# Spacing the operand tiles of three-pass matmuls in SBUF by 80 and 32 bytes

## Chip, cores and metric

The kernel runs as one program on one core of one Trainium2 chip. The metric is the device time of one execution in microseconds, the median of several runs.

## What is computed

The reference chains two transformer blocks over 256 tokens of width 1024, all in float32. The first block has two layers, each with a wide projection, top-k attention and a short convolution, an output mix and an MLP of width 4096 with a squared ReLU. The second has one layer with a windowed and a neighbourhood attention, and then PEER, a product-key retrieval over 128 x 128 experts:

```python
def first_block(...):
    for l in range(DEPTH):                      # 2
        u = rmsnorm(x, norm_mix[l])
        proj = u @ w_in[l]
        ...
        x = x + merged @ w_mix_out[l]
        u = rmsnorm(x, norm_mlp[l])
        x = x + jnp.square(jax.nn.relu(u @ w_mlp_up[l])) @ w_mlp_down[l]
    return rmsnorm(x, norm_final)

def second_block(...):
    ...
    x = x + gate1[:, None, :] * (mixed @ w_out[layer])
    h2 = modulate(rms_norm(x, norm2_g[layer]), shift2, scale2)
    x = x + gate2[:, None, :] * peer(h2, w_query[layer], sub_keys[layer],
                                      u_experts[layer], v_experts[layer])
    return rms_norm(x, final_g)
```

Almost all of the arithmetic is activations (256 tokens) times weights, and every weight is used once.

## The kernel before

**The stream.** All weights are packed on the host into 544 pieces of 128 x 1024 float32 (512 KB each) in the order of use. SyncE loads them into `raw`, a ring of `RING` = 4 slots (L560). For each piece ScalarE writes `w_hi`, the value rounded to the format of TensorE's fast fp32 path (L182), and VectorE writes `w_lo = raw - w_hi` (L187), three pieces ahead of TensorE. `w_hi` and `w_lo` are rings of 4 slots too.

**Three-pass matmuls.** `mm3` (L210 to L212) makes one product of split operands from three matmuls: high by high, high by low, low by high. The activations are split likewise: `u_hi`/`u_lo` hold eight tiles of 128 features x 256 tokens, `a_hi`/`a_lo` two such tiles, used in turn. TensorE meets two forms:

- `piece_b`: a 128 x 128 block of the ring is stationary and a tile of `u` moves, 256 columns, 24 matmuls a piece (8 tiles `k` by 3). The projections, the MLP's up, the queries and the experts' up have this form. The profile writes it as `bank<-u_hi,w_hi` (moving first, then stationary).
- `piece_a`, `expert_down`, `held_pieces`: 128 tokens of `a` (or of `u`, `o`, `mx`) are stationary and half a slot of the ring moves, 512 columns, 12 matmuls a piece. The MLP's down and the experts' down have this form: `bank<-w_hi,a_hi`.

Each matmul carries its own load of the stationary block (LDWEIGHTS, PEld in the profile). The order on every engine is written out by hand and tied by semaphores.

**Where the tiles lie.** The program lays its tiles one after the other in each partition of SBUF, each starting at a multiple of 32 bytes. These are the start addresses in the built program, as remainders by 64 bytes:

| tile | step between its parts, before | start mod 64, before | step, after | start mod 64, after |
|---|---|---|---|---|
| `raw` | 4096 | 0 | 4096 | 0 |
| `w_hi`, `w_lo` (slots 0 to 3) | 4096 | 0, 0, 0, 0 | 4176 | 0, 16, 32, 48 |
| `u_hi`, `u_lo` (tiles 0 to 7) | 1024 | 0 for all | 1056 | 0, 32, 0, 32, ... |
| `a_hi` (2 tiles) | 1024 | 0 | 1024 | 0 |
| `a_lo` (2 tiles) | 1024 | 0 | 1024 | 32 |
| `one_r` | - | 0 | - | 32 |
| `o_hi`, `o_lo`, `y_hi`, `y_lo`, `mx_hi`, `mx_lo` | 1024 | 32 | 1024 | 0 |

`o`, `y` and `mx` are the other activations that meet the ring: attention and convolution outputs before their output projections, and the merged branches. `one_r` is a column of ones that `keep_clock` (L273) multiplies by itself, both operands broadcast.

Of the kernel before, what the change touches and what calls it, by code (L numbers as in the profile page):

```python
# [9 lines left out]
F32R = mybir.dt.float32r  # L10
# [7 lines left out]
P = 128  # L18
T, D = 256, 1024
NT, KD = T // P, D // P  # L20
# [26 lines left out]
PIECE = 1024  # L47
RING = 4
AHEAD = 3
N_LAYER = 59 + 2 * KH  # L50
ADA_GROUPS = 6
ADA_RING = 4
# [2 lines left out]
N_QUERY = 2 * PH  # L55
N_PIECES = LAYERS * N_LAYER + N_MIXER2 + N_QUERY + 2 * PK
SEL_PIECES = 8
# [35 lines left out]
def build(nc, stream, x_in, gains2, gain_cols, conv_w, w_ada, b_ada, c_cols, kept_in, rope_in, na_mask_in,  # L93
          t5_in, t5_hot, rpb_pad, sinks, sub_keys, gain_out, out):
    ctx = ExitStack()
    with ctx:
        def sb(c, name, shape, dt=F32):
            return c.enter_context(nc.sbuf_tensor(name, shape, dt))
# [9 lines left out]


        raw = sb(ctx, "raw", [P, RING, PIECE])  # L110
        w_hi = sb(ctx, "w_hi", [P, RING, PIECE], F32R)
        w_lo = sb(ctx, "w_lo", [P, RING, PIECE], F32R)
        u_hi = sb(ctx, "u_hi", [P, KD, T], F32R)
        u_lo = sb(ctx, "u_lo", [P, KD, T], F32R)
        a_hi = sb(ctx, "a_hi", [P, 2, T], F32R)
        a_lo = sb(ctx, "a_lo", [P, 2, T], F32R)
        kept = sb(ctx, "kept", [P, 2 * P + PT + 2 * LAYERS * KD])
        ident, iota, iota16 = kept[:, 0:P], kept[:, P:2 * P], kept[:, 2 * P:2 * P + PT]
# [53 lines left out]
        def dyn(k):  # L172

            return at["quads"] * k
# [15 lines left out]
        def split(c):  # L190
            split_hi(c)
            split_lo(c)

        def next_piece(last=False):
# [3 lines left out]
            if not last:  # L198
                split(c + AHEAD)
            nc.tensor.wait_ge(s_split, dyn(RING) + (c + 1))  # L200
# [107 lines left out]
        def squares(src, junk, row, marks, tt):  # L308

            for n in range(2):  # L310
                cols = slice(n * 512, (n + 1) * 512)
                m = AC.go((marks[tt][n], junk_mark[0]), S.activation, junk, src[:, tt, cols], ACT.Square,
                          accum_out=st[:, row + n, tt:tt + 1])
                junk_mark[0] = m
            return m
# [18 lines left out]
        def held_pieces(count, lhs, acc, steps, whole=False, ahead=True):  # L334
# [4 lines left out]
            for tt in range(NT):  # L339
                for n in range(2):  # L340
# [10 lines left out]
                    next(steps, None)  # L351
            return list(range(c + AHEAD + 1, c + AHEAD + count))

# [282 lines left out]
        for k, b in enumerate((5, 0, 1, 2, 3, 6, 7, 4)):  # L636
# [6 lines left out]
            u_ready.append((m1, m))  # L643
        for c in range(1, AHEAD):
            split(c)
        for tt in range(NT):
            got_sums[0] = squares(x, space_junk, 5, x_marks, tt)
        for layer in range(LAYERS):
# [422 lines left out]
            if layer < LAYERS - 1:  # L1071
                u_ready, x_sums = added_and_turned(*last_downs, x, gains[:, layer + 1, :], 5, mlp_scale)
                got_sums[0] = squares(x, space_junk, 5, x_sums, 1)
                assert at["piece"] == (layer + 1) * N_LAYER
        ph1a.close()
# [1003 lines left out]
```

## Time and profile before

| | before |
|---|---|
| median of 3 runs | 1732.64 us (1731.53 to 1732.9) |
| span of the profiled execution | 1732.8 us |
| TensorE matmul busy | 1711.1 us, 99% of the span |
| VectorE busy | 1328.8 us, 77% |
| ScalarE busy | 925.9 us, 53% |
| bytes moved by DMA | 327.3 MB, mean 189 GB/s |

The span is that of the execution that the hardware profiler recorded. It stands 0.2 us from the median, so a sum made against the span can be read against the median. Matmuls overlap in the pipeline, so a matmul's duration says little: what counts is the distance between the starts of two that follow each other, here called the pitch.

### The profile page before, as it was taken

The numbers are of one execution on the slowest core, as the hardware profiler recorded it, in microseconds if no ns is written. First come the engines' busy times: TensorE is split into PE (matmuls) and PEld (weight loads), VectorE is DVE, ScalarE is ACT, GpSimd is POOL, SyncE is SP. The second block draws the span as 40 slices with busy tenths as digits, with TensorE's granted clock in tenths as the row PEclk, the third lists the DMA queues.
The fourth block names the chain that finished last, engine by engine and source line by source line (L and its number), as shares of the span: only waits on it lengthen the run. The fifth ranks groups of instructions, "written<-read, shape, count | busy, mean of one in ns | idle before, by whom it ended". The sixth has DMA issues, their size and how long they took to land.

```text
span 1732.8 us, 33390 instructions
## 1 busy us (share of the span) xinstructions
PE 1711.1 (99%) x11670; PEld 1580.1 (91%) x11670; DVE 1328.8 (77%) x2382; ACT 925.9 (53%) x1647; POOL 63.5 (4%) x112
## 2 busy tenths in 40 slices
PE   9999999999999999999999999999999999999997
PEld 8899899989999898999889999999999988888886
DVE  6986778778976787877775999987888766666666
ACT  5444544445454544455554555577777655555553
POOL 0000001000000122100000000000000000000000
PEclk9999999999999999999999999999999999999999
DMA  6556687755445699744344555554444455555554
GB/s 232 170 179 199 217 291 274 244 181 167 162 159 161 226 328 308 253 148 145 122 158 158 166 175 182 182 171 136 145 135 137 144 194 194 193 192 192 191 192 153
DMA packets 90123, 327.30 MB, mean 189 GB/s; under 512 B 11001, under 2 KB 11177, under 8 KB 89585
## 3 DMA queue, kind: packets, MB, share of 16 engines
q1 hardware_dynamic: 79056, 286.45, 49.3%
q0 software_dynamic: 9712, 34.36, 6.2%
q10 hardware_dynamic: 1264, 5.24, 0.8%
q8 instruction: 62, 1.02, 0.2%
q14 instruction: 29, 0.23, 0.0%
HBM read 323.88 MB, written 6.09 MB: 190 GB/s over the span
## 4 chain that ended last, share of the span: by engine, by line
PE 76%; DVE 18%; DMA 2%; issue 2%; ACT 2%; DVEq 0%; ACTq 0%; SPq 0%
PE bank L210 23%; PE bank L211 22%; PE bank L212 22%; DVE Z L87 6%; DVE w_lo L187 6%; PE bank L1769 3%; DMA raw<-stream 1%; DVE yc L87 1%; PE bank L281 1%; PE bank L1310 1%; ACT w_hi L182 1%; PE bank L481 1%; DVE work L87 1%; DVE rot L87 1%; DVE top L87 1%
## 5 line engine op out<-in xcount | busy, mean ns | idle before, releaser
L187 DVE TENSOR_TENSOR w_lo<-raw,w_hi 128x1024 fp32r<-128x1024 f32 x544 | 658.2, 1220 | 162.1 <-ACT w_hi L182 161.2
L182 ACT ACTIVATE w_hi<-raw 128x1024 fp32r<-128x1024 f32 x544 | 572.4, 1054 | 245.5 <-PE bank L212 163.2
L210 PE MATMUL bank<-u_hi,w_hi 128*128 128x256 f32 x2400 | 691.2, 288 | 1.7 <-DVE w_lo L187 0.8
L211 PE MATMUL bank<-u_lo,w_hi 128*128 128x256 f32 x2400 | 679.8, 283 | 0.0
L212 PE MATMUL bank<-u_hi,w_lo 128*128 128x256 f32 x2400 | 679.7, 283 | 0.0
L210 PEld LDWEIGHTS bank<-u_hi,w_hi 128*128 128x128 f32 x2400 | 460.9, 192 | 11.6 <-DVE w_lo L187 3.8
L211 PEld LDWEIGHTS bank<-u_lo,w_hi 128*128 128x128 f32 x2400 | 461.2, 192 | 2.2
L212 PEld LDWEIGHTS bank<-u_hi,w_lo 128*128 128x128 f32 x2400 | 460.7, 192 | 0.0
L210 PE MATMUL bank<-w_hi,a_hi 128*128 128x512 f32 x744 | 290.4, 390 | 0.0
L211 PE MATMUL bank<-w_lo,a_hi 128*128 128x512 f32 x744 | 290.1, 390 | 0.0
L212 PE MATMUL bank<-w_hi,a_lo 128*128 128x512 f32 x744 | 289.5, 389 | 0.0
L212 PEld LDWEIGHTS bank<-w_hi,a_lo 128*128 128x128 f32 x744 | 139.7, 188 | 29.5
L210 PEld LDWEIGHTS bank<-w_hi,a_hi 128*128 128x128 f32 x744 | 139.9, 188 | 27.6 <-issue 0.2
L211 PEld LDWEIGHTS bank<-w_lo,a_hi 128*128 128x128 f32 x744 | 139.9, 188 | 27.0
L1858 ACT ACTIVATE a_hi<-Z 128x256 fp32r (+1 forms) x126 | 52.7, 418 | 169.0 <-PE bank L212 167.2
L1860 DVE TENSOR_TENSOR a_lo<-Z,a_hi 128x256 fp32r<-128x256 f32 x126 | 53.6, 426 | 81.6 <-ACT a_hi L1858 81.6
L1758 ACT ACTIVATE rows_a<-rows_a,sel 128x128 f32<-128x128 f32 x256 | 81.1, 391 | 0.0
L1742 DVE TENSOR_TENSOR rows_a<-kept,sel 128x512 f32<-128x512 f32 x64 | 44.3, 691 | 36.5 <-PE bank L1769 36.4
L1605 ACT ACTIVATE Z<-bank 128x256 f32 (+1 forms) x68 | 26.1, 384 | 79.2 <-PE bank L212 78.9
L959 ACT ACTIVATE qT<-bank 128x256 f32<-128x256 f32 x64 | 24.5, 383 | 74.9 <-PE bank L212 74.7
L994 DVE SCALAR_TENSOR_TENSOR space<-gate,c_tmp,space 128x1024 f32 x42 | 53.8, 1280 | 0.4
L968 DVE CAST a_hi<-qT 128x256 fp32r<-128x256 f32 x60 | 18.0, 300 | 43.9 <-PE bank L212 42.9
(286 smaller groups left out, 1713.1 us busy)
## 6 DMA issues: line engine op xcount, KB each, us to landing
raw<-stream SPq DMA_DIRECT2D x544, 512.0 KB, 3.3
gate<-w_ada POOLq DMA_DIRECT2D x48, 512.0 KB, 6.4
t_rows<-t_by_distance POOLq DMA_DIRECT2D x8, 256.0 KB, 3.4
rpb_rows<-rpb_pad POOLq DMA_DIRECT2D x8, 224.0 KB, 3.9
bias_b<-rpb_rows POOLq DMA_DIRECT2D x16, 96.0 KB, 7.7
bias_a<-t_rows POOLq DMA_DIRECT2D x1, 1536.0 KB, 14.9
x<-x_in ACTq DMA_DIRECT2D x2, 512.0 KB, 5.8
gains_b<-gains POOLq DMA_DIRECT2D x1, 1024.0 KB, 9.0
```

The costliest lines, as they stand in the source:

```text
L87: return self.done(method(*args, **kw))
L182: nc.scalar.activation(w_hi[:, s, :], raw[:, s, :], ACT.Copy).then_inc(s_hi, 1)
L187: nc.vector.tensor_tensor(w_lo[:, s, :], raw[:, s, :], w_hi[:, s, :].bitcast(F32), ALU.subtract).then_inc(s_split, 1)
L210: M.matmul(o, lh, rh, start=start, stop=False, skip_group_check=True)
L211: M.matmul(o, lh, rl, start=False, stop=False, skip_group_check=True)
L212: return M.matmul(o, ll, rh, start=False, stop=stop, skip_group_check=True)
L994: nc.vector.scalar_tensor_tensor(total, ada_raw[:, k % ADA_RING, :], c_act[:, k:k + 1], total, ALU.mult, ALU.add).then_inc(s_ada, 1)
L1742: return V.tensor_tensor(out, iota.unsqueeze(1).to_broadcast([P, GROUP, P]), values.unsqueeze(2).to_broadcast([P, GROUP, P]), ALU.is_equal)
L1758: i = S.activation(rows_a[:, q, e, :], rows_a[:, q, e, :], ACT.Copy, scale=share[:, e:e + 1])
L1769: i = M.matmul(bank[6 + q][:, e * P:(e + 1) * P], rows_a[:, q, e, :], rows_b[q][:, e, :].bitcast(F32), start=True, stop=True, skip_group_c ...
L1858: S.activation(hi[:, q, :], zj, ACT.Copy).then_inc(s_ah, 1)
L1860: V.tensor_tensor(lo[:, q, :], zj, hi[:, q, :].bitcast(F32), ALU.subtract).then_inc(s_al, 1)
```

## The change

Padding is added to five tiles, and the code goes on using the same parts of them. A slot of `w_hi` and `w_lo` takes 80 bytes more, a tile of `u_hi` and `u_lo` 32 bytes more, and `a_hi` 32 bytes more at its end, which moves `a_lo`. All that is allocated behind moves by 1184 bytes. No instruction is added, removed or put elsewhere: the order on each engine is the same, line numbers from L50 on go up by one.

```diff
 RING = 4
 AHEAD = 3
+SLOT_GAP, TILE_GAP = 20, 8
...
         raw = sb(ctx, "raw", [P, RING, PIECE])
-        w_hi = sb(ctx, "w_hi", [P, RING, PIECE], F32R)
-        w_lo = sb(ctx, "w_lo", [P, RING, PIECE], F32R)
-        u_hi = sb(ctx, "u_hi", [P, KD, T], F32R)
-        u_lo = sb(ctx, "u_lo", [P, KD, T], F32R)
-        a_hi = sb(ctx, "a_hi", [P, 2, T], F32R)
+        w_hi = sb(ctx, "w_hi", [P, RING, PIECE + SLOT_GAP], F32R)[:, :, 0:PIECE]
+        w_lo = sb(ctx, "w_lo", [P, RING, PIECE + SLOT_GAP], F32R)[:, :, 0:PIECE]
+        u_hi = sb(ctx, "u_hi", [P, KD, T + TILE_GAP], F32R)[:, :, 0:T]
+        u_lo = sb(ctx, "u_lo", [P, KD, T + TILE_GAP], F32R)[:, :, 0:T]
+        a_hi = sb(ctx, "a_hi", [P, 2 * T + TILE_GAP], F32R)[:, 0:2 * T].rearrange("p (a t) -> p a t", t=T)
         a_lo = sb(ctx, "a_lo", [P, 2, T], F32R)
```

## Rows read from the trace of the kernel before

**Rows 1.** The page: busy time by engine, granted clock, shares of the last chain.

```profile
PE 1711.1 (99%) x11670; PEld 1580.1 (91%) x11670; DVE 1328.8 (77%) x2382; ACT 925.9 (53%) x1647; POOL 63.5 (4%) x112
...
PEclk9999999999999999999999999999999999999999
...
PE 76%; DVE 18%; DMA 2%; issue 2%; ACT 2%; DVEq 0%; ACTq 0%; SPq 0%
```

**Rows 2.** Groups by line and form: count, busy us, mean ns of one, idle before.

```profile
L210 PE MATMUL bank<-u_hi,w_hi 128*128 128x256 f32 x2400 | 691.2, 288 | 1.7 <-DVE w_lo L187 0.8 <-DVE u_lo L87 0.3
...
L210 PE MATMUL bank<-w_hi,a_hi 128*128 128x512 f32 x744 | 290.4, 390 | 0.0
...
L210 PE MATMUL bank<-w_hi,u_hi 128*128 128x512 f32 x120 | 47.6, 397 | 0.1
```

**Rows 3.** TensorE in two stretches of one form each: busy (x matmuls), clock, DMA.

```profile
950.00:980.00 30.00, 30.00 (x253) 1.00 0.50 161
...
1400.00:1500.00 100.00, 100.00 (x443) 1.00 0.58 194
```

**Rows 4.** Timeline of TensorE, output projections: start us, duration us, first and last of 192.

```profile
156.53 0.28 PE L210 MATMUL bank<-o_hi,w_hi 128*128 128x256 f32 x1
...
179.25 0.40 PE L210 MATMUL bank<-w_hi,u_hi 128*128 128x512 f32 x1
```

**Rows 5.** Timeline of TensorE, the merged branches: first and twelfth of a run.

```profile
846.19 0.39 PE L210 MATMUL bank<-w_hi,mx_hi 128*128 128x512 f32 x1
...
848.75 0.39 PE L212 MATMUL bank<-w_hi,mx_lo 128*128 128x512 f32 x1
```

**Rows 6.** Timeline of TensorE, one down piece between up pieces: matmuls 1, 7, 13.

```profile
632.68 0.40 PE L210 MATMUL bank<-w_hi,a_hi 128*128 128x512 f32 x1
...
634.07 0.39 PE L210 MATMUL bank<-w_hi,a_hi 128*128 128x512 f32 x1
...
635.43 0.28 PE L210 MATMUL bank<-u_hi,w_hi 128*128 128x256 f32 x1
```

**Rows 7.** The chain that ended last: a run of broadcast matmuls, start us, us.

```profile
762.96 5.46 PE bank L273 x25
```

**Rows 8.** All engines by stage: PE, PEld, DVE, ACT, POOL busy, clock, DMA share, GB/s.

```profile
589.00:756.00 167.00, 166.61 (x1059) 151.14 (x1058) 132.26 (x186) 75.80 (x97) 30.62 (x49) 1.00 0.88 290
...
955.00:1150.00 195.00, 193.10 (x1597) 191.54 (x1595) 189.00 (x574) 112.72 (x161) 0.00 (x0) 1.00 0.54 180
...
1380.00:1710.00 330.00, 330.00 (x1458) 273.25 (x1457) 199.95 (x244) 166.44 (x244) 0.00 (x0) 1.00 0.57 191
```

**Rows 9.** The ring's two makers, groups by line and form.

```profile
L187 DVE TENSOR_TENSOR w_lo<-raw,w_hi 128x1024 fp32r<-128x1024 f32 x544 | 658.2, 1220 | 162.1 <-ACT w_hi L182 161.2 <-DVE Z L87 0.3
L182 ACT ACTIVATE w_hi<-raw 128x1024 fp32r<-128x1024 f32 x544 | 572.4, 1054 | 245.5 <-PE bank L212 163.2 <-DMA raw<-stream 78.9 <-DVE rows_a L1722 3.0
```

## Prediction

> **What bounds the kernel now.** I read the page first. TensorE is busy 1711.1 us of 1732.8 at full granted clock [rows 1], and the chain that ended last is mostly TensorE. VectorE's 18% of that chain is no room for a rival bound: the chain steps over to VectorE where a wait ended last, but TensorE stands idle for 21.7 us in all. So the time is a sum of matmul pitches, and the question about any change of addresses is whether a pitch moves.
>
> The groups by form [rows 2] give the numbers of matmuls. L210 runs 2400 times with a `u` tile moving (256 columns); L211 and L212 do the same, so 7200. With the ring moving (512 columns) it is (744 + 120) x 3 = 2592. Their mean durations (288 and 390 ns) overlap, so they are no cost. The pitch comes from counting in a stretch of one form [rows 3]. Between 950 and 980 us the count is 253, of which two or three began before the stretch: 30 us / 250 = 120 ns. Between 1400 and 1500 it is 443 less two: 226.8 ns. The reader should see two things. The two pitches differ by 106.8 ns for 256 columns, 0.417 ns a column, which is the 2.4 GHz that the granted clock says. And with the columns taken off, both forms are left with the same surplus: 120 - 106.7 = 13.3 ns, 226.8 - 213.3 = 13.5 ns. The surplus is paid once for each matmul, whatever its length, as a thing would be that belongs to the stationary block's load. Over 9792 matmuls it is 130 us, 7.5% of the span. Only this can change.
>
> **Does the surplus depend on addresses?** The trace has a few places where operands start at other remainders than the ring and `u`, which before are all at 0 by 64 bytes:
>
> - Moving at 32, stationary at 0, 256 columns: the output projections (`o` and `y`), 192 matmuls from 156.53 to 179.25 us [rows 4], 22.72 / 192 = 118.3 ns. That is 1.7 ns less than 120.
> - Moving at 0, stationary at 32, 512 columns: the merged branches, 11 pitches from 846.19 to 848.75 us [rows 5], 232.7 ns. That is 5.9 ns more than 226.8.
> - Both operands broadcast from one address, 512 columns: 5.46 / 25 = 218.4 ns [rows 7], a surplus of 5.1 ns. It is 8.4 ns under the ring's, and reads no successive addresses.
> - All at 0, but just after a change of form: six pitches from 632.68 to 634.07 take 231.7 ns each, the next six, to 635.43, 226.7 ns [rows 6]. The same operand remainders give two prices, so it isn't the remainder alone: a run of equal remainders settles into 226.7 and 120, and what disturbs it costs more in the long form and less in the short one.
>
> I conclude that the stream of the moving operand and the load of the next stationary block disturb each other in SBUF, and that the remainders decide how. The trace shows remainders 0 and 32, never 16 or 48.
>
> **The change part by part.**
>
> *Matmuls with `u` moving, 7200.* In slot 0 the ring stays at 0 and `u` alternates 0, 32 from one `k` to the next, every three matmuls; slot 2 mirrors that; slots 1 and 3 stand 16 or 48 apart. No run of equal remainders is longer than three matmuls, so the settled 120 is not reached. The nearest row is 118.3: 1.7 x 7200 = 12.2 us less. Bounds: nothing gained in the settled state's place, 0; or, since the broadcast run shows that 8.4 ns of the surplus can go, 60 us less. A loss here is bounded by the long form's surplus, +5.9 ns or 42 us, but the only rows of a short form off its settled state are lower, and I keep a tenth of it, +4 us, as my upper end.
>
> *Matmuls with the ring moving, 2592.* The ring moves at 0, 16, 32 or 48, the stationary blocks lie at 0 (`a_hi`) and 32 (`a_lo`), so each pair of slot and block has its own distance, and a run is again never longer than three. A quarter of the pairs are equal, a quarter 32 apart, half at distances that no row shows. Bounds: all of them at the merged branches' price, +5.9 x 2592 = +15.3 us; all at the broadcast run's, -8.4 x 2592 = -21.8 us. The middle of the two is -1.2 ns, and I take -1: -2.6 us. This is a choice between far ends, not a measurement.
>
> *`o`, `y` and `mx`* go from 32 to 0 while the ring goes to mixed remainders. They are 384 + 96 matmuls; at 1.7 ns and 5.9 ns that is at most 1.2 us either way. I put 0.
>
> *Makers of the ring.* `w_hi` takes 1054 ns and `w_lo` 1220 ns [rows 9], 544 times each. Their rows stay contiguous and start at multiples of 16 bytes. A piece lasts 24 x 120 = 2880 ns or 12 x 226.8 = 2722 ns on TensorE, so each maker could grow by 100 ns unseen, save in the stretch from 955 to 1150 us, where VectorE is busy 189.0 of 195 us [rows 8]: some 60 pieces by 100 ns would be 6 us. With nothing in the rows that says they grow, 0.
>
> *Loads.* `raw` stays where it is and moves the same bytes. If TensorE is faster, the ring is asked for earlier. From 589 to 756 us the queues carry 290 GB/s at a busy share of 0.88 [rows 8], and part of a gain there would turn into a wait for DMA. In the stretch up to 1150 us VectorE would take some of it back. Both hold 362 us of the span and 21% of the gain; I give back 2 us.
>
> *Sum.* -12.2 - 2.6 + 2.0 = -12.8 us, from 1732.8 to 1720.0 us. The profiled span lies 0.2 us above the median, so 1719.8 is the same thing for the median; I say 1720.
>
> The Trainium skill speaks against this. TensorE: Matmul & The Clock Gate, part 2, says that TensorE reads SBUF by two independent ports, one for the moving operand and one for LDWEIGHTS, and that loading the next block takes no bandwidth from the running matmul; SBUF — State Buffer, "Who interferes with whom", adds that PE never waits on anyone. By that rule no address matters and the sum is 0. The Trainium skill's TensorE: Matmul & The Clock Gate, "Back-to-back issue gap", has N/2.4 + 2.5 ns, would give 109.2 and 215.8 ns; rows 3 have 120 and 226.8, and rows 4 and 5 differ from them with the remainder, so this trace does not agree with it for this format.
>
> **The rivals.**
>
> *The long form pays (slower), 0.30.* One mechanism: the settled 226.8 of the ring-moving matmuls is lost, and what comes in its place is what rows 5 and the first half of rows 6 show, 231.7 to 232.7 ns. The end stage from 1380 to 1710 us [rows 8] consists of little else. If all 2592 go to 232.7, +15.3; with the short form's 12.2 gained, the kernel stands at 1736; if the short form gains nothing, at 1748. It decides from where the long form's loss per matmul is 12.2 us / 2592 = 4.7 ns, a pitch of 231.5. For it: every row off the settled state in this form is above that. Against it: they are all at distances 0 and 32, and half the new distances are others.
>
> *Nothing happens, 0.14.* The surplus would belong to the format of the load itself, not to where operands lie, and the 1.7 and 5.9 ns of rows 4 and 5 would come from something else that goes with `o` and `mx`. Time: 1732.6 us. This is what the skill's rule would give.
>
> *Most of the surplus goes, 0.08.* The broadcast run's 8.4 ns off each of 9792 matmuls is 82 us, 1651 us. Against it: a stationary load sweeps over successive addresses at its own pace beside a moving stream that does the same, and a constant distance between their starts should not keep them apart all the way.
>
> *My forecast, 0.48:* gains of one to three ns in the short form, about nothing in the long one.
>
> **How the numbers follow.** The likeliest case has its own range from 1700 (the short form at 117, the long one 4 ns lower: -21.6 - 10.4) to 1729. The full range must leave out no more than two in ten. I leave out the large gain and the far end of the slower rival: 1692 to 1744 us. The bound of what a measurement tells from no change is 0.2%, 3.5 us. Faster: 0.46 of the forecast's 0.48, the 0.08, and 0.02 of the slower rival, where the long form's loss stays below 231.5: 0.56. Within 0.2%: 0.14, 0.02 of the forecast and 0.02 of the rival near its threshold: 0.18. Slower: 0.26.
>
> **What would show it.** In the profile after, the counts of rows 3 tell almost everything: 250 matmuls of the short form take 30 us now and should take 29.6; 441 of the long form fill 100 us, and should fill between 99 and 100. The forms may now differ from slot to slot, with a pattern that repeats every four pieces, and from even to odd `k`. If the long form's pitch is above 231 ns, the slower rival is right. If both counts stand, nothing happens. The durations of L182 and L187 (L183 and L188 after) should stand within 10 ns. The prediction is wrong above all if the distances 16 and 48, on which no row speaks, are much better or much worse than 0 and 32.

## The result, and the profile after

The changed kernel takes 1735.28 us in the median of 12 runs (1734.77 to 1736.69), against 1732.64 for the kernel before in 12 runs on the same chip. The ratio is 1.0019, with a 95% interval from 1.0011 to 1.0026: slower by a hair, and 15 us above the forecast. The profiled execution has a span of 1734.3 us.

The page of the kernel after, busy time by engine and the chain that ended last, looks like [rows 1]:

```profile
span 1734.3 us, 33390 instructions
...
PE 1710.3 (99%) x11670; PEld 1569.7 (91%) x11670; DVE 1328.2 (77%) x2382; ACT 926.3 (53%) x1647; POOL 63.3 (4%) x112
...
PE 77%; DVE 18%; issue 2%; ACT 1%; DMA 1%; DVEq 0%; ACTq 0%; SPq 0%
```

Nothing on the page shows that two terms of nearly ten microseconds each have changed sides. The counts do. The first stretch below is that of the short form in [rows 3], which had x253 for 250 pitches; 253 pitches in 30 us are 118.6 ns. The second is another one of mostly 256-column matmuls, which comes back below, and the third has 512-column ones alone; the kernel before has x171 and x443 in these two:

```profile
950.00:980.00 30.00, 30.00 (x256) 1.00 0.51 170
905.00:925.00 20.00, 20.00 (x172) 1.00 0.56 185
1400.00:1500.00 100.00, 100.00 (x433) 1.00 0.56 189
```

The 256-column form (the short form) became a little denser, the 512-column form (the long form) fell from 441 to 431 whole pitches in 100 us, from 226.8 to 232.0 ns. The timeline of TensorE in the experts' down shows the same. Over the twelve pitches from the first row to the second it is 2.79 us, 232.5 ns each:

```profile
1500.12 0.40 PE L211 MATMUL bank<-w_hi,a_hi 128*128 128x512 f32 x1
...
1502.91 0.39 PE L211 MATMUL bank<-w_hi,a_hi 128*128 128x512 f32 x1
```

The groups by line and form, which answer to [rows 2] and [rows 9]: the short form's mean duration fell by 2 ns, the makers of the ring are as they were.

```profile
L211 PE MATMUL bank<-u_hi,w_hi 128*128 128x256 f32 x2400 | 686.7, 286 | 3.3 <-DVE w_lo L188 2.7 <-DVE u_lo L88 0.5
...
L188 DVE TENSOR_TENSOR w_lo<-raw,w_hi 128x1024 fp32r<-128x1024 f32 x544 | 657.7, 1220 | 152.7 <-ACT w_hi L183 152.0 <-DVE Z L88 0.3
L183 ACT ACTIVATE w_hi<-raw 128x1024 fp32r<-128x1024 f32 x544 | 572.4, 1054 | 228.1 <-PE bank L213 169.4 <-DMA raw<-stream 55.0 <-DVE rows_a L1723 3.2
```

**The account.** Below, "pitch" is the mean distance from one start to the next over all matmuls of a form in the whole trace, leaving out distances over 140 ns (short form) and 245 ns (long form), which are waits or other work. The sums include everything. Each pitch is read from one profiled execution; three kernels whose tiles have the same distances (before, move256 and all64 below) agree within 0.1 ns.

| form | matmuls | pitch before | after | sum before, us | after, us |
|---|---|---|---|---|---|
| 256 columns, `u` moves | 7200 | 119.8 | 118.5 | 888.1 | 880.3 |
| 512 columns, `a` stationary | 2232 | 227.4 | 231.6 | 508.4 | 517.0 |
| 512 columns, `u` stationary | 360 | 227.5 | 231.6 | 82.9 | 84.4 |
| `o`, `y`, `mx`, all | 528 | | | 80.8 | 80.6 |

That is -7.8, +8.6, +1.5 and -0.2: +2.1 us, where the span grew by 1.5 and the median by 2.6.

The long form's loss is not the same for all pieces. A piece lies in the slot of its number by 4, and with `a` stationary the pitch after is 229.7, 232.4, 232.8 and 231.7 ns in slots 0 to 3, where before it was 227.4 or 227.5 in each. So there is the pattern over four pieces that the prediction thought possible.

### The profile page after: what moved, and what is told of

Same layout as the page of the kernel before. It is cut to its first block, busy times and chain, and to the rows that moved or that the text cites. A ratio compares the mean times of both kernels' runs of the same rounds, so it can differ in the third digit from the quotient of the medians.

```text
span 1734.3 us, 33390 instructions
## 1 busy us (share of the span) xinstructions
PE 1710.3 (99%) x11670; PEld 1569.7 (91%) x11670; DVE 1328.2 (77%) x2382; ACT 926.3 (53%) x1647; POOL 63.3 (4%) x112
## 4 chain that ended last, share of the span: by engine, by line
PE 77%; DVE 18%; issue 2%; ACT 1%; DMA 1%; DVEq 0%; ACTq 0%; SPq 0%
PE bank L211 23%; PE bank L213 23%; PE bank L212 23%; DVE Z L88 6%; DVE w_lo L188 5%; PE bank L1770 3%; DVE yc L88 1%; PE bank L282 1%; PE bank L1311 1%; PE bank L482 1%; DVE work L88 1%; DVE rot L88 1%; ACT w_hi L183 1%; DVE top L88 1%; DVE rows L88 0%
## 5 line engine op out<-in xcount | busy, mean ns | idle before, releaser
L183 ACT ACTIVATE w_hi<-raw 128x1024 fp32r<-128x1024 f32 x544 | 572.4, 1054 | 228.1 <-PE bank L213 169.4
L211 PEld LDWEIGHTS bank<-u_hi,w_hi 128*128 128x128 f32 x2400 | 453.1, 189 | 12.7 <-DVE w_lo L188 4.3
L212 PEld LDWEIGHTS bank<-u_lo,w_hi 128*128 128x128 f32 x2400 | 453.0, 189 | 2.5
L213 PEld LDWEIGHTS bank<-u_hi,w_lo 128*128 128x128 f32 x2400 | 452.5, 189 | 0.0
L213 PE MATMUL bank<-w_hi,a_lo 128*128 128x512 f32 x744 | 293.2, 394 | 0.0
```

The source lines that it names most:

```text
L183: nc.scalar.activation(w_hi[:, s, :], raw[:, s, :], ACT.Copy).then_inc(s_hi, 1)
L211: M.matmul(o, lh, rh, start=start, stop=False, skip_group_check=True)
L212: M.matmul(o, lh, rl, start=False, stop=False, skip_group_check=True)
L213: return M.matmul(o, ll, rh, start=False, stop=stop, skip_group_check=True)
```

## Experiments

All kernels compute the whole result. They differ from the kernel before only in where the tiles start. Ratios are to the kernel before, timed on the same chip.

**The three parts of the change, and a control.** At this point I had a theory A from rows 3 to 6: a run of matmuls whose operands start at equal remainders by 64 bytes settles at 120 and 226.8 ns, and all else costs 118.4 and 231.6.

*u_gap*, one part of the change alone:

```diff
+        u_hi = sb(ctx, "u_hi", [P, KD, T + 8], F32R)[:, :, 0:T]
+        u_lo = sb(ctx, "u_lo", [P, KD, T + 8], F32R)[:, :, 0:T]
```

> Only u's tiles are spaced by 32 bytes; the ring and a stay. Theory A (a settled pitch needs a run of matmuls in which the moving tile and the next stationary block start at the same remainder by 64 bytes; anything else costs 118.4 ns in the 256-column form and 231.6 ns in the 512-column form, whatever the distance): every 256-column matmul with u at 118.4 instead of 119.8, -10 us; the 360 matmuls with u stationary at 231 instead of 227, +1.4 us; a's stay at 227.4. About 1724 us. Theory B (each pair has the price of its own distance, 120 at 0 and 118.3 at 32): only the odd tiles gain, -6 +1 us, about 1728.

Measured: 1725.9 us, ratio 0.9964 [0.9950, 0.9977]. The short form is at 118.1 ns, the 360 matmuls with `u` stationary at 232.2, `a`'s stay at 227.4. Of the change's three parts this is the one that helps; alone it beats both kernels.

*ring_gap*, the ring's slots alone:

```diff
+        w_hi = sb(ctx, "w_hi", [P, RING, PIECE + 20], F32R)[:, :, 0:PIECE]
+        w_lo = sb(ctx, "w_lo", [P, RING, PIECE + 20], F32R)[:, :, 0:PIECE]
```

> Only the ring's slots are spaced by 80 bytes; u and a stay at 0. Theory A: pieces in slot 0 stay settled (120 and 227), those in slots 1 to 3 go to 118.4 and 231.6: -1.4 x 7200 x 3/4 = -7.5 us, +4.4 x 2592 x 3/4 = +8.6 us, about 1734. Theory B: slot 2 (32 apart) at 118.3 and 232.7, slots 1 and 3 (16 and 48 apart) at prices of their own that may lie anywhere, but constant within a slot.

Measured: 1734.22 us, 1.0011 [1.0002, 1.0021]. Short form 117.9 ns, long form 231.3 with `a` and 231.5 with `u` stationary. So this part by itself brings a gain in the short form and a somewhat larger loss in the long one. The time is theory A's, but the mechanism isn't: pieces in slot 0, which by theory A stay settled at 120 and 227, have 117.2 and 231.1 ns.

*a_lo_off*, `a_lo` 32 bytes off and padded to 64, so that nothing behind it changes its remainder by 64:

```diff
+        a_hi = sb(ctx, "a_hi", [P, 2 * T + 16], F32R)[:, 0:0 + 2 * T].rearrange("p (a t) -> p a t", t=T)
+        a_lo = sb(ctx, "a_lo", [P, 2 * T + 16], F32R)[:, 8:8 + 2 * T].rearrange("p (a t) -> p a t", t=T)
```

> Only a's low part lies 32 bytes off; the ring, u and a's high part stay at 0. Theory A: no run of equal remainders is left in the 512-column form, all 2232 matmuls with a at 231.6 instead of 227.4, +9.4 us, about 1742. Theory B: one matmul in three (the one during which a_lo is loaded) goes to 232.7, +4.4 us, about 1737. The 256-column form stays at 119.8 in both.

Measured: 1742.31 us, 1.0062 [1.0048, 1.0075], short form 119.8, `a`'s long form 232.4. All three of its matmuls pay (6.0, 3.4 and 5.4 ns in the order of `mm3`), not only the one beside which `a_lo` is loaded. This part only costs. The parts don't add up (-6.8, +1.5 and +9.6 by the medians make +4.3, against +2.6), and neither gains nor losses do. By the sums over all distances u_gap and ring_gap each take 9.6 us off the short form, both together with `a_lo` 7.8. In the long form with `a`, ring_gap costs 10.9 us and a_lo_off 10.3, together 8.6.

*gap64*, the control, every step by 64 bytes:

```diff
+        u_hi = sb(ctx, "u_hi", [P, KD, T + 16], F32R)[:, :, 0:T]
+        u_lo = sb(ctx, "u_lo", [P, KD, T + 16], F32R)[:, :, 0:T]
+        a_hi = sb(ctx, "a_hi", [P, 2 * T], F32R)[:, 0:2 * T].rearrange("p (a t) -> p a t", t=T)
+        a_lo = sb(ctx, "a_lo", [P, 2 * T + 32], F32R)[:, 16:16 + 2 * T].rearrange("p (a t) -> p a t", t=T)
```

> A control: u's tiles are spaced by 64 bytes and a's low part lies 64 bytes off, so every address moves, but all remainders by 64 stay 0. Theories A and B: pitches stay at 119.8 and 227.4, time as before, 1732.6 us. Rival C (what matters is any uneven step, at 128 bytes or more too): the pitches change as in u_gap and a_lo_off, 118.4 and 231.6, about 1733.5.

Measured: 1736.3 us, 1.0025 [1.0015, 1.0035], with 118.3 and 231.2 ns. Theory A had given the first three times within 2 us, in ring_gap's case by luck, and this run overturns it: all remainders by 64 are equal here, and both forms are unsettled all the same. The remainder that matters is by more than 64 bytes. The kernels above hid a second sign of it: `o` and `y` move at 118.3 ns where they start 224 bytes off the ring by 256 (before, u_gap), and at 120.0 where 96 bytes off (a_lo_off, gap64); by 128 the two are the same.

**Constant distances.** The next four leave all steps alone and shift `u` and `a` as wholes by dummy allocations of 64, 128, 192 and 256 bytes. By "distance" I mean the start of the moving tile less that of the stationary block, by 256 bytes. A shift of 64 bytes thus gives the short form, where `u` moves, a distance of 64, and the long form, where the ring moves, 192. The diff is move64's:

```diff
+        sb(ctx, "pad_u", [P, 16])
         u_hi = sb(ctx, "u_hi", [P, KD, T], F32R)
...
         a_lo = sb(ctx, "a_lo", [P, 2, T], F32R)
+        sb(ctx, "pad_rest", [P, 48])
```

> u and a as wholes start 64 bytes further on, the ring and all steps as before, so the distance from the ring is constant, 64. Theory D (the distance between moving tile and next stationary block by 256 bytes decides, and only equal remainders settle at 120 and 226.8): pitches of about 118.4 and 231.6, time 1732 to 1735. Theory F (any constant distance settles at 120 and 226.8, a step that isn't a multiple of 256 disturbs): pitches as before, 119.8 and 227.4, 1732.6 us. Theory A with its modulus of 64 is already contradicted by the control.

> The same with 128 bytes. Theory D: about 118.4 and 231.6, 1732 to 1735 us. Theory F: as before, 119.8 and 227.4, 1732.6 us. If the modulus is 128, as before too, and move64 not.

> The same with 192 bytes. Theory D: about 118.4 and 231.6, 1732 to 1735 us. Theory F: as before, 119.8 and 227.4, 1732.6 us.

> The same with 256 bytes. Theories D and F with a modulus of 256: pitches and time as before, 119.8 and 227.4 ns, 1732.6 us. If the pitches change here too, the modulus is larger, or the absolute address counts.

Measured:

| kernel | distances, short / long | time, us | ratio, interval | short form, ns | long form with `a`, ns |
|---|---|---|---|---|---|
| move64 | 64 / 192 | 1737.18 | 1.0029 [1.0019, 1.0039] | 117.6 | 233.4 |
| move128 | 128 / 128 | 1738.18 | 1.0034 [1.0022, 1.0047] | 118.8 | 232.5 |
| move192 | 192 / 64 | 1711.55 | 0.9885 [0.9869, 0.9902] | 114.4 | 229.0 |
| move256 | 0 / 0 | 1732.73 | 0.9999 [0.9990, 1.0009] | 119.8 | 227.4 |

Theory F (any constant distance settles) falls with move64. Theory D's repetition after 256 bytes holds in move256; its single price for everything else does not. At 192 bytes the short form drops to 114.4 ns. That none of the theories had. TensorE in the stretch from 905 to 925 us, of move192 and then of move256:

```profile
905.00:925.00 20.00, 20.00 (x179) 1.00 0.49 162
```

```profile
905.00:925.00 20.00, 20.00 (x171) 1.00 0.52 176
```

The timeline of TensorE in move192, 21 pitches from the first to the last of these rows, 2.38 us, 113.3 ns each:

```profile
959.94 0.28 PE L212 MATMUL bank<-u_hi,w_hi 128*128 128x256 f32 x1
960.05 0.28 PE L213 MATMUL bank<-u_lo,w_hi 128*128 128x256 f32 x1
960.17 0.28 PE L214 MATMUL bank<-u_hi,w_lo 128*128 128x256 f32 x1
...
962.32 0.28 PE L212 MATMUL bank<-u_hi,w_hi 128*128 128x256 f32 x1
```

Not all of it arrives. 5.4 ns by 7200 is 39 us; with the long forms at 229.0 and 229.1 instead of 227.4 and 227.5, 4 us are lost, and of the 35 that remain the median shows 21. The rest is in the distances over 140 ns, which the pitch leaves out: with them the form's sum fell by 26 us, not 39. Some of that is waiting for the ring. TensorE's waits in move192, total us, times, longest, where the kernel before waited 0.8 us for `w_lo` in all [rows 2]:

```profile
PE bank L212 <- DVE w_lo L189: 8.2, 17, 0.9
PE bank L428 <- DVE qT L87: 5.3, 2, 2.7
```

and from 950 to 980 us TensorE stands idle for 0.92 us, 0.9 of them in waits for VectorE's `w_lo`; the kernel before was busy for all 30 us there [rows 3]:

```profile
950.00:980.00 30.00, 29.08 (x254) 1.00 0.61 199
```

**Around the good distance.** Four more kernels, with the same kind of padding (for 16 bytes, a slice that starts four elements into a padded allocation). The diff is u192_a0's:

```diff
+        sb(ctx, "pad_u", [P, 48])
         u_hi = sb(ctx, "u_hi", [P, KD, T], F32R)
         u_lo = sb(ctx, "u_lo", [P, KD, T], F32R)
+        sb(ctx, "pad_a", [P, 16])
```

> Only u starts 192 bytes further on, a 256 (the same remainder by 256 as before). If the distance between moving tile and next stationary block decides by itself in each form: 256-column form at 114.4 as in move192, 512-column form with a at 227.4 as before instead of 229.0. 1711.6 - 1.6 x 2232 = 1708 us. If the two forms influence each other through what a piece of one leaves to the next, either pitch can be lost.

> u at distance 160, a 32 bytes on (distance 224). Distance theory without a closer rule: both forms unsettled, 118.4 and 231.6 within 2 ns, 1730 to 1738 us. If distance 192 is the bottom of a wide dip, 160 is below 118 too, and the time below 1728.

> u at distance 208, 16 bytes behind the good 192; a 240 bytes on (distance 16). If the dip at 192 is wide, u stays below 117 ns; if it is narrow, 118.4. a at 16 bytes from its settled 0: near 227.4 if its dip is wide, 231 to 233 if narrow.

> u at distance 176, a 16 bytes on (distance 240). The same question on the other side: below 117 and near 227.4 if the dips are wide, 118.4 and 231 to 233 if narrow.

| kernel | distances, short / long | time, us | ratio, interval | short form, ns | long form with `a`, ns |
|---|---|---|---|---|---|
| u192_a0 | 192 / 0 | 1711.69 | 0.9878 [0.9862, 0.9895] | 114.9 | 226.8 |
| u160_a32 | 160 / 224 | 1739.05 | 1.0038 [1.0024, 1.0052] | 118.1 | 233.2 |
| u208_a240 | 208 / 16 | 1729.57 | 0.9984 [0.9974, 0.9993] | 118.8 | 228.1 |
| u176_a16 | 176 / 240 | 1743.09 | 1.0057 [1.0041, 1.0074] | 119.2 | 233.0 |

The dip at 192 is narrow: 16 bytes to either side the short form is back at 119. u160_a32 came 1 us above its expected range. u192_a0 missed its expected 1708. The long form did what was expected and a little more (226.8), but the short form lost half a nanosecond against move192, 3.6 us over 7200, and the two nearly cancel. The trace says where: in the first 24 matmuls behind a change of form or a distance over 140 ns the short form has 115.5 ns against 114.7, behind them the two agree at 113.9. That fits with the long form leaving the short one a different start at every change, as in [rows 6]; why it does is open. The long form is good at 0 and passable 16 bytes beyond (ring behind block), bad 16 bytes before. The 360 matmuls with `u` stationary have 229.2 ns at 64 (u192_a0) and add three distances: 230.1 at 80 (u176_a16), 233.3 at 96 (u160_a32) and 232.4 at 48 (u208_a240). So the long form has a second, shallower good place about 64.

**Distance or place?** So far the ring had stood still. These two move it by 64 bytes. The diff is ring64's, where `u` and `a` come 256 bytes further on; all64 has the second pad, of 192 bytes, behind `a_lo`, so that `u` and `a` move by 64 too:

```diff
+        sb(ctx, "pad_w", [P, 16])
         w_hi = sb(ctx, "w_hi", [P, RING, PIECE], F32R)
         w_lo = sb(ctx, "w_lo", [P, RING, PIECE], F32R)
+        sb(ctx, "pad_u", [P, 48])
```

> Only the ring (both parts) starts 64 bytes further on; u and a keep their remainders by 256. Distance theory: u - ring is now 192 and ring - a is 64, the same distances as in move192 with other absolute addresses: 256-column form 114.4, 512-column form 229.0, 1711.6 us, within 2 us for the tiles that lie elsewhere. Absolute theory (what counts is where u and a start): pitches as before, 119.8 and 227.4, 1732.6 us.

> The ring, u and a all start 64 bytes further on, so that all distances between them are 0 as before. Distance theory: pitches as before, 119.8 and 227.4, 1732.6 us. Absolute theory: u and a stand where they stand in move64, 117.6 and 233.4, 1737 us.

ring64 takes 1711.74 us (0.9887 [0.9870, 0.9903]) with 114.7 and 229.0 ns; all64 takes 1732.68 us (1.0001 [0.9992, 1.0011]) with 119.8 and 227.4 ns. TensorE in the two stretches, ring64 first:

```profile
905.00:925.00 20.00, 20.00 (x180) 1.00 0.54 175
1400.00:1500.00 100.00, 100.00 (x438) 1.00 0.59 189
```

```profile
905.00:925.00 20.00, 20.00 (x171) 1.00 0.58 185
1400.00:1500.00 100.00, 100.00 (x443) 1.00 0.59 192
```

Moving the ring alone gives what moving `u` and `a` gave, and moving all three gives nothing. The distance between the operands is shown to be the cause, and the absolute place not, nor the distance from `raw`, which all64 changes. That the pattern repeats by 256 bytes is shown at distance 0 (move256). Two limits remain. A constant distance is the same for the block in the array and for the one being loaded, so these runs can't say which of the two meets the moving tile; a_lo_off, where all three matmuls pay, doesn't single out the next one either. And something else has a small part: at distance 192 ring64 and move192 differ by 0.3 ns, and at 160 `o` and `y` have 117.3 ns (ring64, all64) where `u` has 118.1 (u160_a32).

## Why the prediction was wrong

- *TensorE's pitches are the whole time.* Right. The makers of the ring stayed within 1 ns, the sums of pitches account for the change within 1 us.
- *The short form leaves its settled 120 for 118.3, -12.2 us.* The direction was right, the term was too large. Over the whole trace the form stood at 119.8 before (119.7 in the first 24 matmuls behind a change of form or a distance over 140 ns, 120.0 later) and stands at 118.5 after. That is -9.4 us; the distances over 140 ns grew by 1.6, which leaves -7.8.
- *The long form: "I take -1", -2.6 us.* This step failed. Measured is +4.2 ns with `a` stationary and about +4 with `u`: +10.1 us in the two sums of the account. The term had this form a nanosecond faster, and it lost in all four slots. Every row that showed it off its settled state had 231.7 or 232.7 ns [rows 5, 6], and the middle of two far ends was taken instead, one of which (the broadcast run) isn't a matmul that sweeps over addresses at all. The rule of taking the row that is nearest would have given 231.7, +12.7 us, and 1733.3 before anything is given back. Of the 15.3 us between forecast and result this step has 12.7 and the short form's pitch 2.8.
- *"I give back 2 us"* was about right, as 1.6 us in the short form's distances over 140 ns. TensorE's waits for `w_lo` grew from 0.8 to 2.7 us.
- *`o`, `y`, `mx`: 0.* Right, -0.2 us. The count left out 48 matmuls with `o` stationary, which changes nothing.
- *The slower rival* named place, price and threshold (231.5 ns), and 1736 us where both forms move; 1735.3 came. That the time fits so well is in part luck: both of its terms were larger than what was measured, +15.3 against +10.1 and -12.2 against -7.8 us, and the loss per matmul, 4.2 ns, stayed under its threshold of 4.7. It had 0.30 and should have had most of the chance.
- *"Nothing happens"* had 0.14, and the time alone can't tell it from what happened: +2.6 us lies within the 3.5 us that the prediction called no change. Its mechanism is refuted by the pitches, which moved by -1.3 and +4.2 ns.
- *Remainders by 64 bytes.* Wrong as a rule, and without effect on the sum: gap64 shows that 64 is too small, and move256 that the pattern repeats by 256. In the changed kernel the steps of 80 and 32 bytes put the pairs at many distances. That their prices simply average was not shown.
- *"Distances 16 and 48, on which no row speaks"* were not the surprise: held constant, the long form has 228.1 ns at 16, near its 227.4 at 0, and 232.4 at 48, near the 233.3 of `mx` at 32. In the rows of constant distance the surprise is 192, and it isn't among those that the change holds for longer than three matmuls.
- *The large-gain rival's counter-argument*, that a constant distance can't keep the two streams apart all the way, was too strong: at 192 the short form's surplus over its columns falls from 13.1 to 7.7 ns, with 5.1 in the broadcast run. That the two streams meet in SBUF at all is still only argued.

On the rule that no address matters the runs are clear: the same instructions with the same data take from 1711.6 to 1743.1 us by nothing but the distance between TensorE's two operands. The Trainium skill's SBUF — State Buffer, "Who interferes with whom", has PE never waiting on anyone and calls its two read ports, for the moving operand and for LDWEIGHTS, independent. These runs don't agree with that if it is taken to mean that the place of one operand can't matter to the other; they don't show what happens at the ports. In the Trainium skill's TensorE: Matmul & The Clock Gate, "Back-to-back issue gap", the formula that the prediction compares with is given for an isolated matmul, so the trace's 120 ns against its 109.2 says little about it.

## What to carry to other kernels

In a kernel that TensorE fills with fp32 matmuls that each load their own stationary block, count matmuls in a clean stretch and take the columns off. If a surplus like the 13 ns here is left, shift one operand as a whole against the other by multiples of 64 bytes within 256, and time each. A padded step inside a tile mixes the distances: alone on `u` it gave 6.8 us here, one constant distance 21. Such a shift acts on every form that meets the tile, and here often with opposite signs (at 64 bytes -2.2 and +5.9 ns): price each form by its own rows, and take an unsettled row for an unsettled state, not a midpoint. All of this comes from one kernel, with fp32 operands in TensorE's fast format and 128 x 128 blocks.

## What the runs showed of the hardware

- The pitch depends on the distance, moving tile less stationary block, by 256 bytes. With 256 columns, held constant: 119.8 ns at 0, 117.6 at 64, 120.0 at 96 (`o` and `y`), 118.8 at 128, 118.1 at 160, 119.2 at 176, 114.4 at 192, 118.8 at 208, 118.3 at 224 (`o` and `y`).
- With 512 columns: 227.4 at 0, 228.1 at 16, 233.3 at 32 (`mx`, in the kernel before), 232.4 at 48, 229.0 at 64, 230.1 at 80, 233.3 at 96, 232.5 at 128, 233.4 at 192, 233.2 at 224, 233.0 at 240. The good distances of the two forms are not the same.
- At distance 0 the short form goes at 120.0 ns once it has run for 24 matmuls without a break, and at 119.7 on average before.
- Why the distance matters was not shown, nor whether the two reads meet inside SBUF. No run tried distances that aren't a multiple of 16 bytes.
